# Expert weights loaded as one 16 KB row per partition and one matrix per transfer

## What is computed

```python
N_EXPERTS = 32; TOP_K = 2; D_MODEL = 1024; D_EXPERT = 512
def hierarchical_moe(h, ...):        # twice, once for each of two layers
    ...                              # a group and two of its experts for each token
    def expert_block(args):
        xblk, e = args
        hid = jax.nn.silu(xblk @ w_gate[e]) * (xblk @ w_up[e])
        return hid @ w_down[e]
    ...                              # weighted sum of a token's two experts
```

## Time and profile before

| | us |
|---|---|
| median of three runs | 2727.83 |
| profiled execution, its own time | 2722.21 |
| its span, first to last instruction | 2720.4 |
| TensorE busy | 2502.9 (92%) |
| TensorE weight loads, beside them | 1855.4 (68%) |
| VectorE busy | 1291.9 (47%) |
| DMA, share of 16 engines' time of the main queue | 68.7% |

### The profile page before, as it was taken

The page is one execution under the profiler, slowest core; times in us unless marked ns, Lnnn a source line. Parts: engine busy times, 40 slices in busy tenths (PEclk is TensorE's granted clock), DMA queues, the critical chain, the costliest instruction groups (busy, mean ns, idle before and its releaser), DMA issues.

```text
span 2720.4 us, 39464 instructions
## 1 busy us (share of the span) xinstructions
PE 2502.9 (92%) x16084; PEld 1855.4 (68%) x16085; DVE 1291.9 (47%) x2250; ACT 866.5 (32%) x1475; POOL 298.5 (11%) x382
## 2 busy tenths in 40 slices
PE   5899998998898989998899999989999999989998
PEld 3564433443694433343699888879989988888997
DVE  5554323222665333221454675565465467555545
ACT  2232111110332111110344444444444444444443
POOL 0210010000000010000000212320000011233001
PEclk8999999999998999999999999999999999999999
DMA  9987999999764999999755444335545544334372
GB/s 357 371 346 303 419 419 420 415 420 420 265 235 166 419 419 419 417 420 420 287 201 186 143 133 127 122 124 194 200 164 200 189 136 155 122 112 155 130 240 80
DMA packets 253046, 712.09 MB, mean 262 GB/s; under 512 B 14416, under 2 KB 171744, under 8 KB 196544
## 3 DMA queue, kind: packets, MB, share of 16 engines
q1 hardware_dynamic: 249184, 704.61, 68.7%
q0 software_dynamic: 1616, 2.45, 0.3%
q10 hardware_dynamic: 2064, 2.47, 0.3%
HBM read 705.52 MB, written 1.05 MB: 260 GB/s over the span
## 4 chain that ended last, share of the span: by engine, by line
PE 62%; DMA 21%; issue 6%; DVE 5%; POOL 2%; ACT 2%; SPq 1%; ACTq 0%; DVEq 0%; POOLq 0%
DMA ring<-in_e_w_up_dram 18%; PE w L836 18%; PE w L1095 11%; PE y L878 10%; PE w L840 9%; PE w L1114 2%; DMA ring<-in_ada_w_dram 2%; PE w L1381 2%; PE y L761 1%; PE y L1147 1%; PE w L1366 1%; POOL arena L2783 1%; DVE wsp L1490 1%; SPq L737 1%; DMA xa<-in_x_dram 1%
## 5 line engine op out<-in xcount | busy, mean ns | idle before, releaser
L1490 DVE TENSOR_TENSOR wsp<-ring,wsp 128x1024 fp32r<-128x1024 f32 x470 | 578.7, 1237 | 402.1 <-ACT wsp L1480 401.6
L836 PE MATMUL w<-hh,wsp 128*128 128x256 f32 x4832 | 639.5, 285 | 8.6 <-DVE wsp L1490 8.1
L836 PEld LDWEIGHTS w<-hh,wsp 128*128 128x128 f32 x4832 | 608.7, 192 | 29.5 <-issue 16.0
L1480 ACT CAST wsp<-ring 128x1024 fp32r<-128x1024 f32 x470 | 488.1, 1045 | 394.8 <-PE w L840 218.1
L1095 PE MATMUL w<-ring,arena 128*64 128x512 f32 x2016 | 461.1, 600 | 83.6 <-DMA ring<-in_e_w_up_dram 78.4
L1095 PEld LDWEIGHTS w<-ring,arena 128*64 128x64 f32 x2016 | 155.2, 137 | 351.2 <-issue 349.5
L840 PE MATMUL w<-hl,wsp 128*128 128x256 f32 x2416 | 339.6, 283 | 0.0
L840 PEld LDWEIGHTS w<-hl,wsp 128*128 128x128 f32 x2416 | 312.3, 192 | 0.0
L878 PE MATMUL y<-wsp,zsp 128*128 128x512 f32 x1104 | 267.1, 391 | 3.9 <-DVE wsp L1490 3.8
L1970 DVE TENSOR_TENSOR ht<-w,ht 128x256 f32<-128x256 f32 x64 | 39.5, 618 | 449.2 <-ACT ht L2506 449.2
L2506 ACT ACTIVATE ht<-w 128x256 f32<-128x256 f32 x64 | 40.0, 625 | 634.0 <-PE w L1095 634.0
(11 more groups left out here) (343 smaller groups left out, 2496.2 us busy)
## 6 DMA issues: line engine op xcount, KB each, us to landing
ring<-in_e_w_gate_dram SPq DMA_DIRECT2D x126, 1024.0 KB, 8.6
ring<-in_e_w_up_dram SPq DMA_DIRECT2D x126, 1024.0 KB, 10.8
ring<-in_e_w_down_dram SPq DMA_DIRECT2D x124, 1024.0 KB, 12.1
ring<-in_ffn_in_dram SPq DMA_DIRECT2D x88, 1024.0 KB, 5.5
ring<-in_w_in_dram SPq DMA_DIRECT2D x50, 1024.0 KB, 5.2
ring<-in_ada_w_dram SPq DMA_DIRECT2D x48, 1024.0 KB, 12.0
ring<-in_ffn_out_dram SPq DMA_DIRECT2D x44, 1024.0 KB, 5.1
ring<-in_b_w_in_dram SPq DMA_DIRECT2D x12, 1024.0 KB, 8.6
```

The lines of the kernel that those rows point to most:

```text
L836: pe.matmul(dst, a[:, kc * m:(kc + 1) * m], hh[:, kc, :], start=kc == 0 and j == 0, stop=False)
L1480: ac.copy(shaped(halves(i)[0], u.shape), u.cut(ring[:, u.piece % NSLOT, :])).then_inc(*mark("w_high", i))
L1490: ve.tensor_tensor(shaped(lo, u.shape), u.cut(ring[:, u.piece % NSLOT, :]), shaped(hi, u.shape).bitcast(F32), ALU.subtract).then_inc(*mark ...
```

## The change

Expert weights now come as whole matrices. Partition p holds eight consecutive input features (four inner features for `w_down`), so its row is one run of 16 KB, over two neighbouring slots; one DMA brings 2 MB. For expert e the list has gate, then up, then `w_down` of e-1. Such a piece is issued when both of its slots are free. Exceptions: expert 0 and the last expert's `w_down` keep rows of 8 KB.

`up(e)` multiplies by all of gate first, 16 matmuls of 256 columns, then by all of up, 16 more. The two halves c of the inner features are no longer the first and last 256 columns: c takes columns in neighbouring pairs, 0, 1, 4, 5 and so on for c = 0, so a matmul reads 8 bytes out of every 16. `down` reads `w_down` after the whole matrix has landed and frees both slots at its end. For expert 0 the half from the ring comes before the early half.

The feature order goes from chunks by four to chunks by eight, so the router's part changes with it: `router_shift` has 32 matmuls, against a doubled identity `twice` that VectorE copies first; ScalarE copies twice the columns, and three small GpSimd operations pick the right ones, for which `gathered_half` waits; the split of `vv` reads every eighth feature. A path for experts with over 64 tokens is rewritten alike.

```diff
--- before.py
+++ after.py
@@ want_experts and the list of pieces @@
                 if e_ < E:
-                    wanted.extend(("up", l, e_, h) for h in range(4))
+                    wanted.extend(("up", l, e_, u) for u in range(2))
                 if e_ >= 1:
-                    wanted.extend(("down", l, e_ - 1, h) for h in range(2))
+                    wanted.append(("down", l, e_ - 1))
...
+        def wide_piece(key, src):
+            n = len(pieces)
+            assert n % 2 == 0
+            piece_of[key] = n
+            pieces.append({"wide": src, "units": [], "read": n})
+            pieces.append({"units": [], "read": n})
...
-                _, l, e_, h = w
-                g, u = divmod(h, 2)
-                src = I[("e_w_gate", "e_w_up")[u]][l, e_, 512 * g:512 * g + 512, :]
...
-                pieces.append({"parts": [(lambda r: r, src.rearrange("(p k) n -> p (k n)", p=P))], "units": [],
-                               "read": len(pieces) + 1 - u})
+                _, l, e_, u = w
+                src = I[("e_w_gate", "e_w_up")[u]][l, e_].rearrange("(p k) n -> p k n", p=P)
+                assert e_ or len(pieces) % 2 == u
+                if e_ == 0:
+                    early[l].append((early_up[:, u, :], src[:, 0:4, :], "in_x"))
+                    piece_of[w] = len(pieces)
+                    pieces.append({"parts": [(lambda r: r, src[:, 4:8, :])], "units": [], "read": len(pieces) + 1 - u})
+                else:
+                    wide_piece(w, src)
...
+                elif e_ < E - 1:
+                    wide_piece((*w, 0), src)
+                    piece_of[*w, 1] = piece_of[*w, 0]
+                else:
+                    for h in range(2):
+                        piece_of[*w, h] = len(pieces)
+                        pieces.append({"parts": [(lambda r: r, src[:, 2 * h:2 * h + 2, :])], "units": []})
...
+        def two_slots(s, k):
+            return ring[:, s:s + 2, :].rearrange("p u (k n) -> p (u k) n", k=k // 2)
@@ orders of the features @@
-        def by_four(a):
-            return a.rearrange("p (g q k) -> p g k q", g=2, k=4)
+        def by_eight(a):
+            return a.rearrange("p (q k) -> p k q", k=KC)
...
+        def by_part(a):
+            return a.rearrange("p (q c j) -> p c q j", c=2, j=2)
@@ sync_engine @@
+                if "wide" in piece:
+                    slot_free(n - NSLOT)
+                    slot_free(n + 1 - NSLOT)
+                    sp.dma_start(two_slots(n % NSLOT, piece["wide"].shape[1]), piece["wide"]).then_inc(
+                        *mark(f"ring{n % NSLOT}", n, by=16))
@@ router_shift @@
-                for j in range(4):
-                    for k in range(4):
-                        pe.matmul(o[32 * j:32 * j + 32, :, :, k], ident[:, k::4],
-                                  ab[:, 0:2, :].rearrange("p v (g j) -> p v g j", g=2)[:, :, :, j], start=True, stop=True)
+                for j in range(4):
+                    for k in range(KC):
+                        pe.matmul(o[32 * j:32 * j + 32, :, k, :], twice[:, k::KC],
+                                  ab[:, 0:2, 2 * j:2 * j + 2], start=True, stop=True)
@@ up, on TensorE @@
-                    for h in range(2):
...
-                        r4 = two.rearrange("p u (k n) -> p k u n", k=4)
-                        for k in range(4):
-                            kc = 4 * h + k
-                            for c in range(2):
-                                ins = pe.matmul(b[64 * c:64 * c + 64, :], xg[:, u, kc, x0:x0 + CAP], r4[:, k, :, 256 * c:256 * c + 256],
-                                                start=kc == 0, stop=kc == KC - 1)
+                        for v in range(2):
+                            np_ = piece_of["up", l, e_, v]
+                            pe.wait_ge(*at(f"ring{np_ % NSLOT}", np_))
+                            w = two_slots(np_ % NSLOT, KC)
+                            for kc in range(KC):
+                                for c in range(2):
+                                    ins = pe.matmul(b[64 * c:64 * c + 64, T * v:T * v + T], x(kc), by_part(w[:, kc, :])[:, c],
+                                                    start=kc == 0, stop=kc == KC - 1)
                             ins.then_inc(*mark("ring_read", np_))
@@ down, on TensorE @@
-                        if e_:
+                        if e_ and (h == 1 or np_ != piece_of["down", l, e_, 1]):
                             ins.then_inc(*mark("ring_read", np_))
@@ fold_mix, on VectorE @@
+                ve.tensor_copy(twice.rearrange("p (b n) -> p b n", b=2), ident.unsqueeze(1).to_broadcast([P, 2, P])).then_inc(
+                    *mark("ab", l, "twice"))
@@ moe, on ScalarE @@
-                ac.copy(ab[:, 2:4, :].rearrange("p v k -> p (v k)"), WB[3][:, 64:80]).then_inc(*mark("route_s", "scale", l))
+                ac.copy(both_cols, WB[3][:, 64:96]).then_inc(*mark("route_s", "scale", l))
...
-                    ac.copy(in_chunks(vh[:, t, :]), by_four(vv[:, t, :])).then_inc(*mark("route_s", "v_hi", l, t))
+                    ac.copy(in_chunks(vh[:, t, :]), by_eight(vv[:, t, :])).then_inc(*mark("route_s", "v_hi", l, t))
@@ moe, on GpSimd @@
+                po.tensor_scalar(wide, cols[:, :, 0], const[:, C_ODD:C_ODD + 1], None, ALU.mult).then_inc(*mark("ones", "even", l))
+                po.tensor_scalar(odd_cols, cols[:, :, 1], const[:, C_ODD + 1:C_ODD + 2], None, ALU.mult).then_inc(*mark("ones", "odd", l))
...
+                po.tensor_tensor(wide, wide, odd_cols, ALU.add).then_inc(*mark("ones", "scale", l))
```

More of the change, by code:

```diff
@@ L90, in constants @@
     c[:, C_I5:C_I5 + 512] = np.arange(512)[None, :]
+    for u in range(2):
+        c[:, C_ODD + u] = np.arange(P) // 16 % 2 == u
     return c
@@ L330, in program @@
         bias_rows = ht[:, 0:2, :, :].rearrange("p a b t -> p (a b t)")
+        twice = ht[:, 2, 0, :]
         bias_gated = ht[:, 2:4, :, :].rearrange("p a b t -> p (a b t)")
@@ L700, in late, with slot_free @@
                                     sp.sem_inc(s_, 1)
+            def slot_free(n):
+                if pieces[n]["units"]:
+                    for i in pieces[n]["units"]:
+                        sp.wait_ge(*low_done(i))
+                else:
+                    sp.wait_ge(*at("ring_read", pieces[n].get("read", n)))
             def early_loads(l):
```

135 lines of the change are left out of this document (70 added, 65 removed).

## The result

| | before | after |
|---|---|---|
| median, us | 2727.85 (2727.2 to 2728.15) | 2745.97 (2742.19 to 2749.61) |
| ratio, with its 95% interval | | 1.0070 (1.0057 to 1.0084) |
| profiled execution, its own time | 2722.21 | 2747.24 |
| its span | 2720.4 | 2745.3 |

What follows compares the result with a forecast made beforehand. Bytes through the DMA engines bound two 430 us stretches. Each layer: -8.0 + 1.5 + 0.5 + 1.5 + 0.6 = -3.9 us; two layers -7.8, with 1.4 and 0.6 it is -5.8, so 2722.0 us, range 2711 to 2739.

Steps and rivals of the forecast that it cites:

- faster stream: Two expert stretches of 430 us: 16 KB rows raise the rate 1.9% to 427.5 GB/s, saving 8.0 us for each layer.
- `w_down` in one step: the gap and the tail: For each layer, a 1.5 us gap (0 to 3) behind expert 17 and 1.5 us at the layer's end.
- ring full later: Ahead of 280 us and its like in layer 1: faster stream catches up with the full ring later, losing 0.5 us each.
- passes of 256; pairs: Half products: narrow passes cost 0.13 us more an expert, 0.6 us for each layer; reading in pairs costs 0.
- router: router_shift's extra records cost 1.4 us in layer 0, hidden in layer 1; the doubled identity costs 0.3 us in each layer.
- The steps get coarser: Ring frees and fills in 2 MB steps; with the gap, the later full ring and the tail, 3.5 us for each layer.
- its own failure condition: Forecast altogether wrong if the stream had gaps in the middle of a layer, so a faster rate went into waiting for slots.
- The tail of a layer: Last experts of a layer: `down(30)` starts 1.5 us later, and this reaches the end of the layer.
- The sign of 6.9 us for L1132: Half products: 6.9 us for an expert with nothing to wait for was expected; over 7.3 would say pairs are slow.
- The rival: Half products: reading in pairs makes a pass 20% longer, costing 24 us, so 2746 us; chance 0.11.
- The rule on bandwidth: Loads from HBM bind near 358 GB/s for a core; by this rule the change would leave only its costs.
- The estimate of 1.8% from the ceiling on the other side: Expert stream: from the on-chip memory's 435 GB/s ceiling, 16 KB rows give 1.8%.

Runs made afterwards that it cites:

- run 3: The changed kernel, but every e_w_down comes as two 1 MB transfers with 8 KB rows, each slot freed by itself: 2730.75 us, ratio 1.0021.
- e5_olddown2: Against e1_oldstream: e_w_down comes as one 2 MB issue into two slots, waited for and freed as a whole, rows still 8 KB: 2744.47 us, ratio 1.0069.
- e7_old256: Against e1_oldstream: each pass of 512 columns over gate and up becomes two of 256 in order: 2737.74 us, ratio 1.0048.
- run 12: e7_old256 with another router_shift, one 128 x 128 product instead of the 64 small ones: 2731.09 us, ratio 1.0013.
- e1_oldstream: Also called run 1. Against the changed kernel: expert stream and passes as before; changed router, feature order and constants stay: 2731.41 us, ratio 1.0021.
- run 11: The changed kernel with another router_shift, one 128 x 128 product instead of the 64 small ones, nothing else different: 2745.49 us, ratio 1.0064.

## Why the prediction was wrong

The terms of the sum for both layers, against the pairs of runs:

| term | forecast, us | measured, us |
|---|---|---|
| faster stream | -16.0 | -7.2 for gate and up; a part of `w_down` doesn't show |
| `w_down` in one step: the gap and the tail | +6.0 | +12.5 |
| ring full later | +1.0 | not measured alone |
| passes of 256; pairs | +1.2; 0 | +7.1; +1.6 |
| router | +2.0 | +5.7, with order and constants |
| sum | -5.8 | +19.7 |

**The transfers.** The mechanism was right: fewer packets, a faster stream. The size was too large by a fifth: 1.5% instead of 1.9%. Gate and up in long rows, one issue each, were worth 6 to 8.5 us where two thirds of the 16 us would be 10.7. With the measured 1.5% two thirds are 8.4 us. The third that belongs to `w_down` would be 4 us; its step costs as much with long rows (+13.4) as without (+13.1, +10.9), so no run shows it, and at an uncertainty of 4 us none could.

**The steps get coarser. This step failed.** I asked only at which place in a layer the ring runs short, priced that with 1.5 us and the tail with as much, and took the rest as covered: 6 us for both layers, where three pairs of runs say 11 to 13. Timeline of the kernel after, behind expert 17, as the earlier trace rows:

```profile
494.20 0.33 SPq L756 DMA_DIRECT2D ring<-in_e_w_down_dram  x1
...
496.00 3.59 PE L1193 MATMUL y<-xa,const 128*128 128x512 f32 x8
...
500.67 7.47 PE L1132 MATMUL w<-ring,arena 128*64 128x256 f32 x64
504.60 0.33 SPq L756 DMA_DIRECT2D ring<-in_e_w_gate_dram  x1
```

The transfer issued at 494.20 landed at 505.02, so gate was issued with 0.43 us to go, and its step took 7.40 us instead of 4.91: a gap of 2.5 us, within my 0 to 3. In layer 1 the like took 2.8. But 27 more issues had leads below 4.3 us, with 12 us between them. The reason is a row that I had read for its place only. When the last byte of `w_down` lands, halves leave TensorE half of `down` still to do, 1.8 us; the whole matrix leaves all of it, 3.65 us; the 44.7 us ahead of L1151 are TensorE waiting for that byte. There are 44 such waits, for 60 matrices that come whole. No slot of `w_down` comes free in that time, so the issues behind come later all through the layer and not at one place. Halves instead of the whole moved gate's median lead from 4.6 to 5.7 us (run 3). The text named its own failure condition, a stream with gaps in the middle of a layer, and gave it no chance and no time. It was a rival with a price: 11 to 13 us, by three pairs of runs. The price is shown. That it is paid through the lead is argued from the 17.3 us at short leads in the kernel after, and holds at most in part for `e5_olddown2`, where 4.4 us stand there.

**The tail of a layer** came as worked out. In the kernel after, `down(30)` starts 5.18 us behind the second half of `up(31)`, 3.46 before, 1.7 us for my 1.5:

```profile
698.01 3.84 PE L1132 MATMUL w<-ring,arena 128*64 128x256 f32 x32 [0.96 <-DMA ring<-in_e_w_up_dram]
703.19 3.65 PE L1151 MATMUL w<-ring,ht 128*64 128x512 f32 x16 [1.33 <-DMA ring<-in_e_w_down_dram]
```

**Half products.** The 4 ns for a narrow pass were about 1 ns: sixteen of them took 3.67 us (`e7_old256`), the eight wide ones 3.65. The time still grew by 7 us where the sum had 1.2. That is the second term that failed: it counted TensorE's time alone, and took the instructions themselves, and their code, as free. The overlap with packets of code (run 12) is the candidate; the cause stays open. The sign of 6.9 us for L1132 was set wrongly, too: 7.09 plus 0.13 is 7.2, as a row runs to the end of its last matmul. In order it took 7.13, in pairs 7.47. Pairs I took at 0; they cost 5% of a pass. The rival priced them from 20% and said that below some 10% they are hidden for the most part, and so it was: 1 to 2 us. That the same rival named 2746 us, the time that was measured, is chance: its mechanism brought 1 to 2 of the 24 us that it stood for. By the Trainium skill, "SBUF — State Buffer", in "Door 1: The DMA port swizzle", two reads out of a 16-byte line are enough for full speed. The passes read in pairs took 3.82 us for 3.65, so in this kernel the rule misses by 5%.

**The router.** The kernel after in layer 0, TensorE and VectorE, as the earlier trace rows:

```profile
189.53 0.82 DVE L1565 COPY ht<-const 128x256 f32<-128x256 f32 x1
...
198.19 3.26 PE L831 MATMUL w<-ab,ht 128*32 128x4 f32 x61
```

3.26 us less 1.27 is 2.0, where 32 records at 44 ns were to be 1.4; each took 53 ns. The doubled identity took 0.82 us, not 0.35. In layer 1 I called the router hidden because of one wait of 1.95 us behind it. It cost 2.8 us there in `e1_oldstream` and 2.1 in the kernel after. A wait downstream covers only what is off the path to it; TensorE's clock, at half for 27.3 us there in `e1_oldstream` and 23.9 in the kernel after instead of 20.5, may have a share. Together 5.7 us instead of 2.0, by the ratio of run 1, which has the order of features and the constants in it as well. The split at every eighth feature was right at 0: the four casts took 2.06 to 2.09 us against 2.03 to 2.07 before, one of them in the earlier trace rows. No engine is seen waiting for the three operations on GpSimd.

**The rule on bandwidth.** By the Trainium skill, "DMA: Bandwidth & Descriptors", in "Where 436 GB/s comes from", loads from HBM are bound near 358 GB/s, which would leave no gain from rows. The windows at 428 and 429 GB/s say again that it does not bind here. The estimate of 1.8% from the ceiling on the other side was close to the measured 1.5%.

## What to carry to other kernels

A ring of buffers has two measures, its bytes and its step. If the step doubles in a full ring, follow one slot around: when does its last reader finish, counted from the landing of its last byte, and how far does the queue reach from there? Do it for every matrix, not only for the place where the ring is shortest. A gain in rate of 1.5% is worth nothing if the lead of the issues shrinks by a quarter, and the dips in the GB/s of narrow slices show that at once.

Change the length of a row, the step of the ring, the width of a pass and the order of columns one at a time. Count the instructions of a version beside their busy time: here twice the matmuls cost 7 us at the same busy time. Of the change one part gained 7 us and four lost; the version with long rows only where their step doesn't hurt, and a cheaper router, takes 2722.6 us, but the one without long rows is as fast.

## What the runs showed of the hardware

A row of 16 KB is worth 1.5% over one of 8 KB: 2 MB in 4.91 us against 4.98, 427 against 421 GB/s. The lead that a step needs was not the same each time: at a lead of 2.5 us a step was unharmed before and 1.1 to 1.2 us too long twice in `e1_oldstream`, at 0.4 us it was 2.5 us too long. Steps of transfers also lengthen by 0.3 to 1.5 us at leads of 5 to 10 us, 2 to 10 us in all for a kernel; 63 of 77 us of this, over twelve traces, stand at the 568 steps of 3001 that a packet of code overlaps. TensorE's clock fell to half in mid-layer behind waits of 2.1 to 2.7 us for a transfer (1084 us in the kernel after, 491 and 1119 in run 11, 419 and 1041 in run 12), and stayed there for 3.4 us. A matmul that reads 8 of each 16 bytes takes 5% longer. And twice as many matmuls of half the width cost 7 us here, while their records add up to the same time.
